# State-space stage of a two-layer encoder: its products in two halves of the array's columns, the swapped input as a second product, and the block loop in another order

## What is computed

```python
def s5_mixer(h, lam_re, lam_im, log_step, b_re, b_im, c_re, c_im, d_skip, w_glu):
    u = h.astype(f32).reshape(bsz, seq, S5_GROUPS, S5_GROUP)     # 64 groups of 16 channels
    lam_bar = jnp.exp(lam * step)                                # 64 complex states a group
    b_bar = ((lam_bar - 1.0) / lam)[..., None] * b
    bu = lax.complex(einsum('gpc,bsgc->bsgp', real(b_bar), u),
                     einsum('gpc,bsgc->bsgp', imag(b_bar), u))
    _, states = lax.associative_scan(combine, (a, bu), axis=1)   # x_t = lam_bar x_{t-1} + bu_t
    y = einsum('gcp,bsgp->bsgc', c_re, real(states)) - einsum('gcp,bsgp->bsgc', c_im, imag(states))
    y = y.reshape(bsz, seq, D_MODEL) + d_skip * h
    y = jax.nn.gelu(y)
    z = y @ w_glu
    return z[..., :D_MODEL] * jax.nn.sigmoid(z[..., D_MODEL:])
```

## Time and profile before

| | us |
|---|---|
| median of 3 runs | 1801.21 (1799.46 to 1801.22) |
| the profiled execution | 1800.29 |
| its span, first to last instruction | 1798.5 |
| TensorE busy | 1779.8 (99%) |
| VectorE / ScalarE / GpSimd busy | 931.6 / 641.4 / 306.9 |
| block loop of the state-space stage | 408.7 to 454.5 |
| granted TensorE clock, mean | 0.998 |

### The profile page before, as it was taken

The page is one execution under the profiler, slowest core; times in us unless marked ns, Lnnn a source line. Parts: engine busy times, 40 slices in busy tenths (PEclk is TensorE's granted clock), DMA queues, the critical chain, the costliest instruction groups (busy, mean ns, idle before and its releaser), DMA issues.

```text
span 1798.5 us, 21542 instructions
## 1 busy us (share of the span) xinstructions
PE 1779.8 (99%) x8142; PEld 1459.5 (81%) x8142; DVE 931.6 (52%) x1107; ACT 641.4 (36%) x868; POOL 306.9 (17%) x268
## 2 busy tenths in 40 slices
PE   8999999999999999999999999999999999999998
PEld 6888788889888888888888888888866788888887
DVE  7777968747555334433374344333664554444333
ACT  6232232347434333332253333222454433333222
POOL 8884615016014000000000000000100200000000
PEclk9999999999999999999999999999999999999999
DMA  5345555588422222232223222222410332322221
GB/s 195 111 153 145 159 150 148 164 302 318 135 94 96 103 94 93 97 102 94 94 82 108 102 93 93 98 101 94 123 36 1 106 105 95 103 94 93 97 91 48
DMA packets 80979, 207.25 MB, mean 115 GB/s; under 512 B 24049, under 2 KB 34417, under 8 KB 79889
## 3 DMA queue, kind: packets, MB, share of 16 engines
q1 hardware_dynamic: 69664, 189.86, 31.9%
q0 software_dynamic: 2784, 14.29, 2.3%
q10 hardware_dynamic: 8464, 2.20, 0.5%
HBM read 183.25 MB, written 23.07 MB: 115 GB/s over the span
## 4 chain that ended last, share of the span: by engine, by line
PE 91%; DVE 4%; ACT 2%; issue 2%; DMA 1%; SPq 1%; POOL 0%; ACTq 0%; DVEq 0%
PE bank L1614 28%; PE bank L1616 28%; PE bank L1615 28%; PE bank L1943 1%; DVE w_split L1158 1%; PE bank L1924 1%; PE bank L1926 1%; PE bank L1791 1%; PE bank L1808 1%; PE bank L1801 1%; PE bank L1686 1%; ACT w_split L748 1%; PE bank L1935 0%; DMA x_res<-xT 0%; PE bank L1644 0%
## 5 line engine op out<-in xcount | busy, mean ns | idle before, releaser
L1158 DVE TENSOR_TENSOR w_split<-w_raw,w_split 128x1024 fp32r<-128x1024 f32 x296 | 388.4, 1316 | 618.0 <-ACT w_split L748 617.2
L1614 PE MATMUL bank<-h_split,w_split 128*128 128x512 f32 x1504 | 589.5, 392 | 4.6 <-DVE w_split L1329 2.7
L1616 PE MATMUL bank<-h_split,w_split 128*128 128x512 f32 x1504 | 585.7, 389 | 0.0
L1615 PE MATMUL bank<-h_split,w_split 128*128 128x512 f32 x1504 | 585.6, 389 | 0.0
L748 ACT ACTIVATE w_split<-w_raw 128x1024 fp32r<-128x1024 f32 x296 | 311.9, 1058 | 635.8 <-PE bank L1616 626.8
L1614 PEld LDWEIGHTS bank<-h_split,w_split 128*128 128x128 f32 x1504 | 282.4, 188 | 66.3 <-DVE w_split L1329 3.2
L1615 PEld LDWEIGHTS bank<-h_split,w_split 128*128 128x128 f32 x1504 | 282.5, 188 | 59.2 <-issue 1.4
L1616 PEld LDWEIGHTS bank<-h_split,w_split 128*128 128x128 f32 x1504 | 282.4, 188 | 58.9
L1614 PE MATMUL bank<-g_split,w_split 128*128 128x512 f32 (+1 forms) x854 | 328.4, 385 | 0.1
L1616 PE MATMUL bank<-g_split,w_split 128*128 128x512 f32 (+1 forms) x854 | 327.8, 384 | 0.0
L1615 PE MATMUL bank<-g_split,w_split 128*128 128x512 f32 (+1 forms) x854 | 327.8, 384 | 0.0
(11 more groups left out here) (287 smaller groups left out, 1198.1 us busy)
## 6 DMA issues: line engine op xcount, KB each, us to landing
w_raw<-wstream SPq DMA_DIRECT2D x296, 512.0 KB, 3.5
op_slot<-s_ops SPq DMA_DIRECT2D x5, 2048.0 KB, 10.5
s_ops<-ops_out SPq DMA_DIRECT2D x16, 512.0 KB, 3.1
op_slot<-s_ops POOLq DMA_DIRECT2D x3, 2048.0 KB, 14.2
s_ops<-c_pow POOLq DMA_DIRECT2D x8, 512.0 KB, 5.3
s_ops<-k_window SPq DMA_DIRECT2D x64, 64.0 KB, 3.4
x_res<-xT SPq DMA_DIRECT2D x8, 256.0 KB, 7.5
s_u<-x_gained ACTq DMA_DIRECT2D x8, 256.0 KB, 5.9
```

The costliest lines, as they stand in the source:

```text
L1158: tt(W[:, r, 1, :], RAW[:, r, :], W[:, r, 0, :].bitcast(F32), ALU.subtract).then_inc(s_lo, 1)
L1614: mm(bank, hi, x_hi, start=start, stop=True, skip_group_check=True)
L1615: mm(bank, hi, x_lo, start=False, stop=True, skip_group_check=True)
L1616: return mm(bank, lo, x_hi, start=False, stop=True, skip_group_check=True)
```

## The change

Each product of the stage is issued as two halves (`strips`): output partitions 0 to 63 and 64 to 127, each with 64 columns of the operator, at column positions 0 and 64 of TensorE's array. `swap_input` is gone; in its place `step_input(k, True)` is a second product, with the two halves of the operator exchanged, into bank 2 + k % 2. TensorE's order becomes: 0, swapped 0, 1, swapped 1, taps 0, 2, taps 1, swapped 2, then per block `step_input(k + 3)`, `from_states(k)`, a filler (`strips_warm`, 256 columns in two halves), swapped `step_input(k + 3)`, `from_inputs(k + 2)`; in the last blocks there are more `keep_warm`. On ScalarE the order per block is `copy_s(k + 2)`, `gelu(k - 1)`, `swap_state(k)`, `r_of_steps(k + 1)`, and y_hi(0) and y_hi(1) follow the last block, with y_hi(2) and y_hi(3) behind gelu(7). VectorE scales u(0) and u(1), GpSimd u(2) and u(3) ahead of input_cos(0); y_lo(0) follows the last block. SP issues operators 4 and 5 ahead of u(7).

```diff
--- before.py
+++ after.py
@@ -492,10 +492,11 @@
             load_u(4)
             sp.wait_ge(s_used, FFN0A2 + 3 * HALF)
             sp.dma_start(op_slot(3), ops_dram[3]).then_inc(s_slot[3], 16)
-            for k in range(5, DT):
+            for k in (5, 6):
                 load_u(k)
             for k in (4, 5):
                 sp.dma_start(op_slot(k), ops_dram[k]).then_inc(s_slot[k], 16)
+            load_u(DT - 1)
             for k in (6, 7):
                 sp.wait_ge(s_yp, k - N_SLOTS + 1)
@@ -682,10 +683,9 @@
                 cos(ZC, ZS[k % 2][:], k).then_inc(s_zc, 1)
             pool.wait_ge(s_rstd, N_S5 + 1)
-            scale_u(1)
             scale_u(2)
+            scale_u(3)
             input_cos(0)
-            scale_u(3)
             input_cos(1)
             for k in range(BLOCKS):
                 state_cos(k)
@@ -916,12 +916,6 @@
                 nc.scalar.activation(dst[0:64, :], src[64:P, :], ACT.Copy)
                 return nc.scalar.activation(dst[64:P, :], src[0:64, :], ACT.Copy)
-            def swap_input(k):
-                if k >= 2:
-                    act.wait_ge(s_z, k - 1)
-                swap_halves(BK[2 + k % 2], BK[k % 2]).then_inc(s_js, 1)
             def swap_state(k):
                 act.wait_ge(s_z, k + 1)
                 if k >= 2:
@@ -940,21 +934,18 @@
             for k in range(2):
                 copy_s(k)
-                swap_input(k)
             for k in range(BLOCKS):
+                if k + 2 < BLOCKS:
+                    copy_s(k + 2)
+                if k >= 1:
+                    gelu(k - 1)
                 swap_state(k)
                 if k + 1 < BLOCKS:
                     r_of_steps(k + 1)
-                if k >= 1:
-                    gelu(k - 1)
-                if k + 2 < BLOCKS:
-                    copy_s(k + 2)
-                    swap_input(k + 2)
-                else:
-                    y_hi(2 * (k - 6))
-                    y_hi(2 * (k - 6) + 1)
+            y_hi(0)
+            y_hi(1)
             gelu(BLOCKS - 1)
-            for k in range(4, DT):
+            for k in range(2, DT):
                 if k == DT - 2:
                     split(GLU, 2 - AHEAD)
                 y_hi(k)
@@ -1370,8 +1361,10 @@
             link(ts(RT[:], RT[:], 1.0 / D, EPS, ALU.mult, ALU.add))
             nc.vector.reciprocal(RT[:], RT[:]).then_inc(s_rcp, 1)
             dve.wait_ge(s_rstd, N_S5 + 1)
-            dve.wait_ge(s_uld[0], 16)
-            tt(UY[:, 0:GB, :], UY[:, 0:GB, :], RT[:].unsqueeze(1).broadcast_to([P, GB, STEPS]), ALU.mult).then_inc(s_un0, 1)
+            for k in range(2):
+                dve.wait_ge(s_uld[k], 16)
+                uk = UY[:, k * GB:(k + 1) * GB, :]
+                tt(uk, uk, RT[:].unsqueeze(1).broadcast_to([P, GB, STEPS]), ALU.mult).then_inc(s_un0, 1)
             split(GLU, 1 - AHEAD)
             def turn_input(k):
@@ -1412,10 +1405,8 @@
                 scan(k)
                 if k + 1 < BLOCKS:
                     turn_input(k + 1)
-                else:
-                    y_lo(0)
                 turn_state(k)
-            for k in range(1, DT):
+            for k in range(DT):
                 if k == DT - 2:
                     split(GLU, 2 - AHEAD)
                 y_lo(k)
@@ -1774,23 +1765,37 @@
             pe.wait_ge(s_sq, SQ_OF[N_S5] + DT)
             mm(total[:], ONES[:], SQ[:, (DT - 1) % 2, :], start=False, stop=True, skip_group_check=True).then_inc(s_ssq, 1)
-            def group(ap, g, n=P):
-                return ap[:, g * n:(g + 1) * n]
-            def step_input(k):
+            def strips(bank, g, ops, rhs, start, swapped=False):
+                for q in range(2):
+                    side = slice(64 * q, 64 * q + 64)
+                    o = 64 * (1 - q if swapped else q)
+                    last = mm(bank[side, g * STEPS:(g + 1) * STEPS], ops[:, g * P + o:g * P + o + 64], rhs,
+                              start=start, stop=True, skip_group_check=True, tile_position=(0, 64 * q))
+                return last
+            def strips_warm(bank):
+                for q in range(2):
+                    mm(bank[64 * q:64 * q + 64, 0:2 * P], ONES[:, 0:64], ONES[:].unsqueeze(1).broadcast_to([P, 2, P]),
+                       start=True, stop=True, tile_position=(0, 64 * q))
+            def step_input(k, swapped):
                 ops = op_slot(k)
-                if k == 0:
-                    pe.wait_ge(s_un0, 1)
-                else:
-                    pe.wait_ge(s_un, k)
-                pe.wait_ge(s_slot[k], 16)
-                if k >= 2:
-                    pe.wait_ge(s_js, k - 1)
+                if not swapped:
+                    if k < 2:
+                        pe.wait_ge(s_un0, k + 1)
+                    else:
+                        pe.wait_ge(s_un, k - 1)
+                        pe.wait_ge(s_sc, k - 1)
+                    pe.wait_ge(s_slot[k], 16)
+                elif k >= 2:
+                    pe.wait_ge(s_z, k - 1)
                 for g in range(GB):
-                    last = mm(group(BK[k % 2], g, STEPS), group(ops[:, O_B:O_B + 1024], g), UY[:, k * GB + g, :],
-                              start=(g == 0), stop=True, skip_group_check=True)
-                last.then_inc(s_s, 1)
+                    last = strips(BK[2 * swapped + k % 2], g, ops[:, O_B:O_B + 1024], UY[:, k * GB + g, :], g == 0, swapped)
+                last.then_inc(s_js if swapped else s_s, 1)
             def from_inputs(k):
                 ops = op_slot(k)
@@ -1798,35 +1803,42 @@
                     pe.wait_ge(s_y, k - 1)
                 for g in range(GB):
-                    mm(group(BK[4 + k % 2], g, STEPS), group(ops[:, O_T:OPS], g), UY[:, k * GB + g, :],
-                       start=(g == 0), stop=True, skip_group_check=True)
+                    strips(BK[4 + k % 2], g, ops[:, O_T:OPS], UY[:, k * GB + g, :], g == 0)
             def from_states(k):
                 ops = op_slot(k)
                 pe.wait_ge(s_xs, k + 1)
                 for g in range(GB):
-                    last = mm(group(BK[4 + k % 2], g, STEPS), group(ops[:, O_C:O_T], g), XS[:, k % 2, g, 0:STEPS],
-                              start=False, stop=True, skip_group_check=True)
+                    last = strips(BK[4 + k % 2], g, ops[:, O_C:O_T], XS[:, k % 2, g, 0:STEPS], False)
                 last.then_inc(s_yp, 1)
             keep_warm(4, BK[7])
             pe.wait_ge(s_zero, 1)
-            step_input(0)
-            step_input(1)
+            for k in range(2):
+                step_input(k, False)
+                step_input(k, True)
             from_inputs(0)
-            step_input(2)
-            keep_warm(1, BK[5])
+            step_input(2, False)
             from_inputs(1)
+            step_input(2, True)
             for k in range(BLOCKS):
+                if k + 3 < BLOCKS:
+                    step_input(k + 3, False)
                 from_states(k)
                 if k + 3 < BLOCKS:
-                    step_input(k + 3)
+                    pe.wait_ge(s_sc, k + 3)
+                    strips_warm(BK[k % 2])
+                    step_input(k + 3, True)
+                    from_inputs(k + 2)
                 elif k < BLOCKS - 1:
-                    pe.wait_ge(s_js, BLOCKS)
+                    pe.wait_ge(s_sc, BLOCKS)
                     keep_warm(1, BK[0])
-                if k + 2 < BLOCKS:
-                    from_inputs(k + 2)
+                    if k + 2 < BLOCKS:
+                        from_inputs(k + 2)
+                        keep_warm(1, BK[0])
+                    else:
+                        keep_warm(2, BK[0])
             first_pair(GLU, 0, G, lambda k: pe.wait_ge(s_y_lo, k + 1))
```

## The result

The changed kernel took 1803.76 us in the median of 20 runs (1801.27 to 1809.13), the kernel before 1800.20 (1798.99 to 1802.15) in as many: a ratio of 1.0024 with a 95% interval of 1.0017 to 1.0030. It is slower, by a quarter of a per cent, where the forecast was 1797.0 and faster. The profiled execution has a span of 1801.8 us, against 1798.5.

What follows compares the result with a forecast made beforehand. TensorE, by its weight loads, was taken to bound the stage loop; state(0) 0.4 us earlier and periods of 4.51 instead of 5.36 start the GLU 3.9 us sooner: 1796.4, or 1797.3 by median; forecast 1797.0, range 1795.5 to 1814.

Steps and rivals of the forecast that it cites:

- The halves: TensorE's stage products: two column halves run nearly fully beside each other, 0.93 us per product instead of 1.79.
- p: Time of one stage product in halves on TensorE: taken as 0.93 us, between 0.89 and 1.79.
- turns: Rival on TensorE's products: halves take turns, p = 1.79, 8.01 us per block, +19 to +21 us; chance 0.17.
- part overlap: Rival on TensorE's products: p 1.0 to 1.15, -2 to +1 us, chance 0.12; 1.15 to 1.6, +1 to +13, 0.10.
- serial work: Rival on TensorE: loads don't run beside matmuls of other halves, 3.3 us per product, +70 us; chance 0.03.
- the fifth: Rival on TensorE's filler: its halves don't pair, 4.59 us a block, 0.4 us of gain gone; no chance given.
- The ring: Stage loop, state to state through TensorE, ScalarE and VectorE: from_states, gelu, swap copies, turn; p + 3.58 = 4.51 us.
- The start: Stage's first blocks: state(0) at 417.81 instead of 418.18, a gain of 0.4 us.
- The sum: Whole stage: state(0) plus seven periods of 4.51, GLU start at 450.36 instead of 454.29, 3.9 us less.
- rival (4): TensorE's instruction fetch over full transfer engines, or a lowered clock: +1 to +6 us over the forecast; chance 0.05.
- The clock: TensorE in blocks 5 and 6: new idle stretches of 0.9 and 1.0 us might lower the clock; within rival (4).
- The cover of y and slot 7: GLU start and block 7: late y_hi(2), y_lo(2) covered by 0.4 us; slot 7 landing at 432, needed near 435.

Runs made afterwards that it cites:

- After: The changed kernel, with halves, fourth product and new orders, all transfers kept: 1803.76 us, ratio 1.0024 to the kernel before.
- e6: The kernel before with only its three products cut in halves, swap_input on ScalarE and all orders kept: 1796.4 us, 4.0 us faster than the kernel before.
- e1: The changed kernel without the transfers of operators 3 to 7, blocks 3 to 7 reading those of blocks 0 and 1: 1798.20 us against 1800.47.
- before: The unchanged kernel, with three full-array products per block and swap_input on ScalarE: 1800.20 us in the median of 20 runs.
- e3: The changed kernel with SP issuing u(7) ahead of operators 4 and 5 again, as in the kernel before: stage 49.51 us, against 49.66.
- e11: The halves alone (e6) with from_inputs(k + 2) issued twice in the loop, for the instruction count of four products: 3.4 us slower than e6.
- e12: The changed kernel with all transfers, gelu(k - 1) moved behind swap_state(k) on ScalarE: 1803.03 us.
- e4: The changed kernel plus three 2 MB memory-to-memory copies on GpSimd's queue in blocks 3 to 5: 9.9 us slower than without the copies.
- e2: The kernel before without the transfers of operators 3 to 7, blocks 3 to 7 reading those of blocks 0 and 1: time stays where it was.
- e5: The kernel before plus three 2 MB memory-to-memory copies on GpSimd's queue in blocks 3 to 5: 16.2 us slower than without the copies.
- e8: The changed kernel without operator transfers 3 to 7 and with gelu(k - 1) behind swap_state(k) on ScalarE: stage 42.17 us, against 43.62.
- e10: The halves alone (e6) with ScalarE's loop in the changed kernel's order, swap_input(k + 2) last: periods 7.4 to 7.6 us for five blocks.

## Why the prediction was wrong, step by step

**The halves: right.** The step on which all hung, p = 0.93 us with 1.79 as the far end. After, a product of 32 stands in the timeline with 1.15 us and two in a row with 2.04 to 2.09, so one adds 0.89 to 0.94; e6 shows what they alone bring. The doubt of the Trainium skill that the prediction quoted ("TensorE: Matmul & The Clock Gate", "Part 3: Packing small matmuls — row/col tiling": loads overlap only with another row group) is not borne out: both halves use all rows, and a load and a matmul together cost 0.93/32 = 29 ns. The rivals of turns, part overlap and serial work are out, and the fifth too: after's filler starts at 438.77 and the next product at 439.21, so its four matmuls take 0.44 us, in pairs.

**The ring: right, a little small.** Forecast p + 3.58 = 4.51, measured 4.60. Its links after:
```profile
442.00 0.69 DVE L1394 TENSOR_TENSOR state<-state_cos,bank 128x512 f32<-128x512 f32 x1
...
443.95 0.60 ACT L928 ACTIVATE u_and_y<-bank 128x512 f32<-128x512 f32 x1 [1.13 <-PE bank L1773]
...
444.57 0.59 ACT L916 ACTIVATE bank<-state_turned 64x512 f32<-64x512 f32 x1
...
445.17 0.60 ACT L917 ACTIVATE bank<-state_turned 64x512 f32<-64x512 f32 x1
...
445.87 0.70 DVE L1389 TENSOR_TENSOR bank<-bank,op_slot 128x512 f32<-128x512 f32 x1 [0.46 <-ACT bank L917]
...
446.61 0.69 DVE L1394 TENSOR_TENSOR state<-state_cos,bank 128x512 f32<-128x512 f32 x1
```
VectorE started 0.10 us after the second copy's end, not 0.04; the rest is as summed. What I did not ask is whether the ring was needed: it is longer than VectorE's own 4.18, and e6 shows that ScalarE keeps its two copies of swap_input and still fits beside VectorE. Once the halves had freed TensorE, the fourth product bought nothing.

**The start: too early by 0.8 us.** State(0) was forecast 9.1 us after the first step input and came at 9.92 in e1. VectorE's weight split took 2.23 us instead of 1.77, and then VectorE waited 0.63 us for GpSimd's first input_cos: the two scalings ahead of it took GpSimd 3.47 us, after 3.00 in before, and its two input_cos 3.50. "Nothing is later there" did not hold.

**The sum without transfers.** Start +0.8, seven periods +1.0 (six of 4.60 and one of 4.95 instead of 4.51), the last product +0.15: 43.6 us against 41.7, which is e1's 43.62. By this the change would have brought about 2 us, and did: 1798.20 against 1800.47. These sizes make up 2.0 of the 8.0 us by which the stage missed its forecast.

**TensorE's supply of instructions: the step that failed.** The sum has no term for it; it stands only in rival (4), "Feeding or clock", at a chance of 0.05. What the runs showed in its place: TensorE used up a block of instructions before the next was there, because with the transfer engines full its packet started only 3.0 to 3.9 us after the block had been entered. ("I cost the move at zero" meant SP's order alone, and that held: undone in e3, it left the stage at 49.51.) Between e1 and after lie 6.0 us of stage: the first state 1.0 us later and the periods 5.0 us longer. Against 4.61, the periods are longer by 1.56 us from state(0) to (1) (standstill 1.31), by 1.77 from (2) to (3) (1.57), and by 1.99 from (3) to (4), where the clock of 0.50 made from_states(3) start 1.2 us after its state (437.29 against 436.09). The rival named the mechanism, 64 instructions per 0.93 us over full transfer engines, and its +1 to +6 us are close to what it cost, +5.6 in the median; but the earlier trace rows had the transfer share at 1.01 and the number of instructions was known, and I let the pages of before, in which nothing stood still, speak for it. There each pair took 112 ns; the halves ask for one every 29. That the measured time still lies within the stated range is luck: its upper end stood for halves that overlap in part, which they did not do, and not for this.

**The clock: half right.** The idle time before from_states, which I feared, never lowered it in after or e1 (1.15 us at most), but the standstills did, one time of three; and in e6 2.88 us of idle did. Neither is a rule: in e11 the same idle stretch of 2.87 us and in e12 a standstill of 2.77 us left the clock at 1.00.

**The cover of y and slot 7.** Neither cost anything. The GLU started behind from_states(7) with no wait for y_lo. Slot 7 was forecast for 432 and landed at 438.6 (issued at 426.3, when the late from_states(1) was done, 12.3 us under way); its product came at about 441, late itself through the standstills.

**What is shown and what is not.** Shown: the standstills need both the transfers (e1 against after, e4) and the number of instructions on TensorE (e6 against e11; e2, e5 for before); each ends 2.2 to 2.5 us after a packet of TensorE's instructions has started, at fixed places of its program; and the packets start late where the transfer share is near 1.0. The new ring costs 1.45 us of stage (e8). Not shown: what in the transfer engines holds a packet back for 3 to 4 us, what fills the 1.4 us or so between the end of most packets and TensorE's going on, and why one standstill lowers the clock and another does not.

## What to carry to other kernels

A product whose moving side is shorter than its weight load gains by being cut into column halves, but count the instructions per microsecond that come out of it, and look at the transfer share of the same stretch: where that is near 1.0, a block of 256 instructions must last longer than the next one takes to come, here some 6.2 us. Take the part of a change that frees the bound engine alone first, and see what is bound then; here the other parts paid for room that was no longer wanted. A step that moves one engine's work ahead of a copy must be walked through the queues of both neighbours, as e10 shows.

## What the runs showed of the hardware

Fp32 matmuls of 64 stationary and 64 moving columns, two halves side by side over all rows, go at 29 ns for a load and a matmul, against 112 ns for 128 stationary columns: 1.92 times a product's rate. TensorE's instructions came in packets of 16 KB, one per 256; a packet started 0.2 to 1.4 us after TensorE had entered a block where the transfers were thin (e1) and 3.0 to 3.9 us after it at a share near 1.0 (after), and the next block could run 2.2 to 2.5 us after the packet's start. Where a block was used up sooner, TensorE stood still, released by nothing, for up to 2.8 us, and some but not all of these standstills put the clock to 0.50 for about 3 us. And a store of 256 KB behind 4 MB of loads took 17.5 us to land.
